# Twenty-two unused f32 products on TensorE ahead of the wait for the ranks

## The chip, the cores and the metric

The kernel runs on one core of one Trainium2 chip. The metric is the device time of one execution in microseconds (us); lower is better. The median of three runs of the kernel before is 2611.15 us (2604.75 to 2613.42).

## What is computed

Two models run one after the other on 512 tokens of width 1024. The first has two layers (attention beside a convolution, then an expert-choice mixture), the second one layer. The change lies in the mixture of the first model, so it runs twice per execution:

```
logits = jnp.einsum('bsd,de->bse', h, w_router).astype(jnp.float32)
aff = jax.nn.softmax(logits, axis=-1)
gate, idx = lax.top_k(aff.transpose(0, 2, 1), cap)      # 16 experts, 64 tokens each
xe = jax.vmap(lambda hb, ib: hb[ib])(h, idx)
hid = jax.nn.silu(jnp.einsum('becd,edf->becf', xe, w_gate)) * jnp.einsum('becd,edf->becf', xe, w_up)
ye = jnp.einsum('becf,efd->becd', hid, w_down) * gate[..., None].astype(h.dtype)
return zeros((S, D)).at[idx].add(ye)
```

All weights and the activations are f32.

## The kernel before

`layer` (L288) writes one program per engine; a loop on the device runs it twice (`nc.Fori(0, DEPTH)`, L2862). Engines meet at semaphores, and the order on each engine is the order in which the code is written. No planner is involved.

The token tile `xT` holds the tokens as 128 features by 512 tokens, eight tiles deep, in f32. After the output projection and the router's logits, TensorE transposes `xT` in eight groups of four (`turn_rows`, L772), so that ScalarE can write the tokens row by row (`htok_ev`, L1038 and L1039), and it transposes the affinities (L779, `affT_done`). On VectorE the top 64 tokens of each of 16 experts are then found in eight rounds of the eight largest values (L1299, L1301), numbered by a scan (L1306) and masked (L1308, `rank_ready`). TensorE waits for `rank_ready` (L783), transposes the ranks with four small products (L785, `rankT_done`), and VectorE builds from them the one-hot matrix of the first pair of experts (`build`, L1313, `s_built`). With it TensorE gathers the tokens of that pair: `gather(0)` is 16 matmuls, alternately of L795 and L796, 8 for each half of the width. `gates(0)` (L810, L812) and `turn_tokens(0)` (L804) follow, VectorE scales and shifts the result (L1327, L1329), and the first expert starts (`expert`, L837 for gate and up, L864 for down).

The weights of an expert come in six chunks of 2 MB on SyncE's one queue (L446). Eight chunks are issued before the first expert starts: six of expert 0 and two of expert 1. Each further one waits for `chunk_used`, which TensorE signals after every chunk (`expert`, for the first time after the first four products of both halves). PSUM bank 0 is read last by L1274 before this place, and is written next by `gather(0)`.

Line names for matmuls: the operand marked `fp32r` or named `_r` is a rounded f32; `ident` (in the tensor `const`) and `xT` are plain f32. In the profile one L795 or L796 matmul is one record; the plain f32 product of the convolution's sum, L737 (four per layer, `ones` by `acc`, 128x512), is of the same kind and shape as the products of the change.

Of the kernel before, what the change touches and what calls it, by code (L numbers as in the profile page):

```python
# [14 lines left out]
KT = D // P  # L15
# [272 lines left out]
def layer(nc, A, sem, M, l, ahead):  # L288


    ps, const, xT, ring, scr = M["ps"], M["const"], M["xT"], M["ring"], M["scr"]
    ident, rot = const[:, C_IDENT:C_IDENT + P], const[:, C_ROT:C_ROT + P]
# [118 lines left out]
    with nc.Block() as block:  # L411
# [98 lines left out]
        def _(pe):  # L510
# [255 lines left out]
            def turn_rows(i):  # L766
                t, g = i // 2, i % 2
                if i >= 4:
                    pe.wait_ge(htok_ev, i - 3)
                for b in range(4):  # L770
                    kt = 4 * g + b
                    mm = pe.transpose(ps[:, 2 + i % 4, b * P:(b + 1) * P], xT[:, kt, t * P:(t + 1) * P], ident)  # L772
                mm.then_inc(htok_mm, 1)
# [6 lines left out]
            mm.then_inc(affT_done, 1)  # L780
            for i in range(4, 2 * TT):
                turn_rows(i)
            pe.wait_ge(rank_ready, 1)  # L783
            for t in range(TT):
                mm = pe.transpose(ps[:, 7, t * EXPERTS:(t + 1) * EXPERTS], rankm[:, t * P:(t + 1) * P].bitcast(F32), ident[0:EXPERTS, 0:EXPERTS])  # L785
# [2136 lines left out]
```

## Time and profile before

| | us |
|---|---|
| median of three runs | 2611.15 |
| the profiled execution's own time | 2608.86 |
| its span | 2607.0 |
| TensorE busy | 2362.6 (91%) |
| VectorE busy | 1134.7 (44%) |
| ScalarE busy | 911.7 (35%) |
| DMA, mean over the span | 250 GB/s |
| TensorE clock, mean granted share of full speed | 0.973 |

Busy time is the sum over an engine's instructions; matmuls overlap at their ends, so that the distance between two starts, and not a duration, is what one costs in a dense row. A clock of 1.00 is 2.4 GHz, 0.50 is 1.2 GHz.

### The profile page before, as it was taken

The page shows a single profiled execution, that of the slowest core. Times are in us where ns is not written, and L with a number is a line of the kernel's source. Part 1 is how long each engine was busy: PE and PEld are TensorE (multiplying, and loading weights), DVE is VectorE, ACT ScalarE, POOL GpSimd, SP SyncE. Part 2 cuts the span into 40 slices and gives each one's busy share as a digit, 9 for nine tenths or more (in the row PEclk, how much of TensorE's full clock was granted, in tenths as well). Part 3 has the DMA queues.
Part 4 walks back from the last instruction along what each step waited for, and adds up shares of the span by engine and source line. Part 5 has one row for each costly group of instructions (what it writes and reads, how often), then busy time and mean ns, then how long its engine had stood idle before and what let it go on. Part 6 is the DMA issues. An engine that isn't in the chain of part 4 may idle for free. (4 is left out here: it accounts for less than half of the span.)

```text
span 2607.0 us, 31029 instructions
## 1 busy us (share of the span) xinstructions
PE 2362.6 (91%) x12565; PEld 1482.3 (57%) x12565; DVE 1134.7 (44%) x1678; ACT 911.7 (35%) x1228; POOL 241.9 (9%) x114
## 2 busy tenths in 40 slices
PE   6999799888887999799888888999999899989997
PEld 5735533333335835543333328887788777767776
DVE  4984312111214984321112125656612112458997
ACT  3256211111114256211111116656622234247775
POOL 0000100000000000100000005000244322200000
PEclk8999899999998989899999999999999999989999
DMA  9702499999999503399999995423123421149995
GB/s 347 277 1 100 159 388 409 410 410 410 410 408 356 211 0 119 153 409 409 410 410 409 410 405 166 162 81 97 65 85 89 133 76 54 49 159 379 369 372 215
DMA packets 276595, 650.47 MB, mean 250 GB/s; under 512 B 12144, under 2 KB 110718, under 8 KB 276222
## 3 DMA queue, kind: packets, MB, share of 16 engines
q1 hardware_dynamic: 272756, 637.98, 65.1%
q0 software_dynamic: 2592, 7.87, 0.8%
q10 hardware_dynamic: 1130, 2.99, 0.3%
q8 instruction: 83, 1.36, 0.2%
q14 instruction: 34, 0.28, 0.0%
HBM read 641.99 MB, written 8.39 MB: 249 GB/s over the span
## 5 line engine op out<-in xcount | busy, mean ns | idle before, releaser
L837 PE MATMUL ps<-ring,hy 128*64 128x512 f32 x992 | 225.6, 596 | 49.7 <-DMA ring<-in_w_up 32.2
L837 PE MATMUL ps<-ring,scr 128*64 128x512 f32 x992 | 225.2, 596 | 37.3 <-DMA ring<-in_w_up 31.3
L1343 DVE TENSOR_TENSOR scr<-scr,ps 128x512 f32<-128x512 f32 x32 | 22.0, 687 | 541.2 <-PE ps L837 541.2
L864 PE MATMUL ps<-ring,scr 128*64 128x512 f32 x1024 | 227.2, 595 | 4.1 <-ACT scr L1054 2.7
L1609 POOL TENSOR_TENSOR raw_r<-raw,w_high 128x2048 fp32r<-128x2048 f32 (+1 forms) x38 | 164.6, 4342 | 463.5 <-ACT w_high L1876 463.5
L1631 PE MATMUL ps<-x_high,w_high 128*128 128x512 f32 x464 | 187.4, 404 | 7.3 <-DVE y L2272 7.3
L2752 DVE TENSOR_TENSOR ring_r<-ring,ring_high 128x2048 fp32r<-128x2048 f32 x77 | 173.0, 2285 | 28.3 <-ACT ring_high L2629 28.2
L1633 PE MATMUL ps<-x_high,raw_r 128*128 128x512 f32 x464 | 184.5, 398 | 0.0
L837 PEld LDWEIGHTS ps<-ring,hy 128*64 128x64 f32 x992 | 69.2, 137 | 202.3 <-issue 122.4
L1632 PE MATMUL ps<-xT_r,w_high 128*128 128x512 f32 x464 | 183.5, 396 | 0.0
L837 PEld LDWEIGHTS ps<-ring,scr 128*64 128x64 f32 x992 | 68.1, 137 | 188.4 <-issue 121.1
L1131 DVE SCALAR_TENSOR_TENSOR one_hot_T<-h_tok,convw,one_hot_T 128x512 f32<-128x512 f32 x240 | 166.3, 745 | 1.8
L2629 ACT ACTIVATE ring_high<-ring 128x2048 fp32r<-128x2048 f32 x77 | 144.0, 1917 | 31.8 <-DMA ring<-in_w_up 31.1
L864 PEld LDWEIGHTS ps<-ring,scr 128*64 128x64 f32 x1024 | 70.5, 137 | 141.1 <-issue 128.8
L1876 ACT ACTIVATE w_high<-raw 128x2048 fp32r<-128x2048 f32 (+1 forms) x58 | 105.9, 1826 | 96.2 <-DMA raw<-in_p_b 49.0
L1063 ACT ACTIVATE hy<-ps,gcol 64x512 f32<-64x512 f32 x64 | 43.6, 682 | 256.3 <-PE ps L864 255.9
L1631 PEld LDWEIGHTS ps<-x_high,w_high 128*128 128x128 f32 x464 | 87.8, 189 | 29.5 <-DVE y L2272 7.7
L1632 PEld LDWEIGHTS ps<-xT_r,w_high 128*128 128x128 f32 x464 | 87.9, 189 | 22.7 <-issue 2.2
L1633 PEld LDWEIGHTS ps<-x_high,raw_r 128*128 128x128 f32 x464 | 87.6, 189 | 19.5
L2542 PE MATMUL ps<-ring_high,xg_high 128*128 128x512 f32 x224 | 92.9, 415 | 2.9 <-DVE xg_low L2758 2.9
L1054 ACT ACTIVATE scr<-ps 128x512 f32<-128x512 f32 x32 | 19.1, 595 | 206.2 <-PE ps L849 206.2
L2544 PE MATMUL ps<-ring_high,xg_low 128*128 128x512 f32 x224 | 87.8, 392 | 0.0
(581 smaller groups left out, 4520.4 us busy)
## 6 DMA issues: line engine op xcount, KB each, us to landing
ring<-in_w_up SPq DMA_DIRECT2D x64, 2048.0 KB, 23.6
ring<-in_w_down SPq DMA_DIRECT2D x64, 2048.0 KB, 23.5
ring<-in_w_gate SPq DMA_DIRECT2D x60, 2048.0 KB, 23.3
ring<-in_w_up SPq DMA_DIRECT2D x56, 1024.0 KB, 6.9
ring<-in_w_ada SPq DMA_DIRECT2D x22, 2048.0 KB, 13.7
ring<-in_w_down SPq DMA_DIRECT2D x28, 1024.0 KB, 6.6
raw<-in_w_in SPq DMA_DIRECT2D x24, 1024.0 KB, 5.0
raw<-in_w_in SPq DMA_DIRECT2D x20, 512.0 KB, 5.2
```

The costliest lines, as they stand in the source:

```text
L837: mm = pe.matmul(ps[CAP * half:CAP * (half + 1), 1 + j // 2, :], x_e[j % 2][:, at_x:at_x + CAP], weights[:, k, half * HALF:(half + 1) * HA ...
L864: mm = pe.matmul(ps[CAP * half:CAP * (half + 1), 4, :], hidT[:, at_f:at_f + CAP], weights[:, k, half * HALF:(half + 1) * HALF], start=(j = ...
L1131: op = dve.scalar_tensor_tensor(acc[:, c, :], src, w, acc[:, c, :], ALU.mult, ALU.add)
L1609: pool.tensor_tensor(dst, src, high.bitcast(F32), ALU.subtract).then_inc(w_ready, 1)
L1631: pe.matmul(out, s_high, m_high, start=(n == 0), stop=False)
L1632: pe.matmul(out, s_high, m_low, start=False, stop=False)
L1633: mm = pe.matmul(out, s_low, m_high, start=False, stop=(n == len(terms) - 1))
L1876: act.activation(slot_of(w_high, n), landed_chunk(n), ACT.Copy).then_inc(w_split, 1)
L2542: pe.matmul(ps[:, n % 2, :], xh[i % 2][:, kt, :], h[:, k, :], start=(kt == 0), stop=False)
L2544: mm = pe.matmul(ps[:, n % 2, :], xl[i % 2][:, kt, :], h[:, k, :], start=False, stop=(kt == KT - 1))
L2629: act.activation(high[q], raw[q], ACT.Copy).then_inc(w_split, 1)
L2752: dve.tensor_tensor(low[q], raw[q], high[q].bitcast(F32), ALU.subtract).then_inc(w_ready, 1)
```

## The change

Between the last `turn_rows` and the wait for the ranks, TensorE is given 22 products, `ident` as the stationary matrix and a token tile as the moving one, each whole in itself, into PSUM bank 0. Nothing reads their result and no semaphore is signalled.

```
             for i in range(4, 2 * TT):
                 turn_rows(i)
+            for i in range(22):
+                pe.matmul(ps[:, 0, :], ident, xT[:, i % KT, :], start=True, stop=True)
             pe.wait_ge(rank_ready, 1)
             for t in range(TT):
                 mm = pe.transpose(ps[:, 7, t * EXPERTS:(t + 1) * EXPERTS], rankm[...], ident[0:EXPERTS, 0:EXPERTS])
```

## Rows read from the trace of the kernel before

**Rows 1.** The page's head and its first part: busy time by engine.
```profile
span 2607.0 us, 31029 instructions
PE 2362.6 (91%) x12565; PEld 1482.3 (57%) x12565; DVE 1134.7 (44%) x1678; ACT 911.7 (35%) x1228; POOL 241.9 (9%) x114
```
**Rows 2.** Timeline of TensorE, first layer: start, length, what, idle before it.
```profile
295.18 0.60 PE L779 MATMUL ps<-const,aff 128*16 128x128 f32 x4 [0.99 <-DVE aff L1293]
295.62 0.64 PE L772 MATMUL ps<-const,xT 128*128 128x128 f32 x4
...
299.07 0.66 PE L772 MATMUL ps<-const,xT 128*128 128x128 f32 x4 [0.50 <-ACT one_hot_T_r L1039]
310.19 0.60 PE L785 MATMUL ps<-const,krg_r 16*128 16x16 f32 x4 [10.47 <-DVE krg_r L1308]
311.67 0.77 PE L795 MATMUL ps<-one_hot_T_r,scr_r 128*128 128x512 f32 x1 [0.87 <-DVE scr_r L1313]
312.23 0.63 PE L796 MATMUL ps<-h_tok_r,scr_r 128*128 128x512 f32 x1
312.66 0.63 PE L795 MATMUL ps<-one_hot_T_r,scr_r 128*128 128x512 f32 x1
...
317.76 0.39 PE L795 MATMUL ps<-one_hot_T_r,scr_r 128*128 128x512 f32 x1
317.99 0.40 PE L796 MATMUL ps<-h_tok_r,scr_r 128*128 128x512 f32 x1
318.23 0.95 PE L810 MATMUL ps<-aff,scr_r 128*128 128x2 f32 x8
...
321.70 3.65 PE L837 MATMUL ps<-ring,scr 128*64 128x512 f32 x16 [1.07 <-DVE scr L1329]
```
**Rows 3.** Timeline of VectorE at the same place.
```profile
309.46 0.68 DVE L1308 TENSOR_TENSOR krg_r<-hy 16x512 fp32r<-16x512 f32 x1
310.83 0.69 DVE L1313 TENSOR_TENSOR scr_r<-const,ps 128x512 fp32r<-128x512 f32 x1 [0.70 <-PE ps L785]
```
**Rows 4.** Timeline of TensorE, second layer.
```profile
1078.30 0.66 PE L772 MATMUL ps<-const,xT 128*128 128x128 f32 x4 [0.50 <-ACT one_hot_T_r L1039]
1089.42 0.60 PE L785 MATMUL ps<-const,krg_r 16*128 16x16 f32 x4 [10.46 <-DVE krg_r L1308]
1090.90 0.77 PE L795 MATMUL ps<-one_hot_T_r,scr_r 128*128 128x512 f32 x1 [0.87 <-DVE scr_r L1313]
...
1096.99 0.95 PE L810 MATMUL ps<-aff,scr_r 128*128 128x2 f32 x8
```
**Rows 5.** Windows: length, busy by engine, PEclk, DMA share, GB/s.
```profile
290.00:299.00 9.00, 5.42 (x58) 3.87 (x50) 5.22 (x17) 7.13 (x14) 3.37 (x3) 1.00 0.95 363
300.00:302.00 2.00, 0.00 (x0) 0.00 (x0) 1.90 (x5) 2.00 (x5) 2.00 (x3) 0.66 1.01 403
317.00:318.00 1.00, 1.00 (x5) 0.78 (x4) 0.00 (x0) 0.00 (x0) 0.00 (x0) 0.64 0.00 0
1082.00:1084.00 2.00, 0.00 (x0) 0.00 (x0) 1.91 (x4) 0.96 (x3) 2.00 (x3) 0.58 1.03 410
1095.00:1096.00 1.00, 1.00 (x4) 0.81 (x3) 0.00 (x0) 0.28 (x1) 0.00 (x0) 0.52 0.00 0
```
**Rows 6.** Timeline of TensorE at the convolution's sum, first layer, full clock.
```profile
194.20 3.60 PE L737 MATMUL ps<-one_hot_T,ones 128*128 128x512 f32 x8
197.64 1.02 PE L707 MATMUL ps<-ring 128*128 128x512 f32 x2
```
**Rows 7.** Groups by line and form: names, shapes, count, busy us, mean ns, idle.
```profile
L795 PE MATMUL ps<-one_hot_T_r,scr_r 128*128 128x512 f32 x128 | 54.9, 429 | 1.7 <-DVE scr_r L1313 1.7
...
L737 PE MATMUL ps<-one_hot_T,ones 128*128 128x512 f32 x16 | 7.2, 592 | 0.0
```
**Rows 8.** Timeline of SyncE's queue, 311 to 326 us: all that it issued.
```profile
325.40 0.37 SPq L446 DMA_DIRECT2D ring<-in_w_up  x1
```
**Rows 9.** Windows after the wait and in the loop of experts, columns as in rows 5.
```profile
320.00:322.00 2.00, 0.93 (x8) 0.59 (x8) 1.74 (x3) 0.32 (x1) 0.00 (x0) 1.00 0.00 0
...
480.00:520.00 40.00, 34.84 (x158) 12.58 (x154) 9.43 (x18) 5.42 (x8) 0.00 (x0) 1.00 1.03 410
```
**Rows 10.** Waits of SyncE's queue, 300 to 345 us: total, times, longest.
```profile
SPq L446 <- PE ps L837: 40.5, 4, 31.6
```

More of the change, by code:

```diff
@@ L782, in _ @@
                 turn_rows(i)
+            for i in range(22):
+                pe.matmul(ps[:, 0, :], ident, xT[:, i % KT, :], start=True, stop=True)
             pe.wait_ge(rank_ready, 1)
```

## Prediction

> **What bounds the kernel now.** I read the page's busy times first [rows 1]: TensorE is busy for 91% of the span, so anything that keeps it longer in one place is likely to be paid. An average says nothing about this place, so the next view is TensorE's timeline around the edit [rows 2]. The reader is to see there a hole: the last group of token transposes starts at 299.07, the next instruction, the transposes of the ranks, at 310.19, after 10.47 us of idle time that VectorE's L1308 ended. VectorE's timeline [rows 3] has L1308 ending at 309.46 + 0.68 = 310.14. In the second layer the hole is the same, 10.46 us [rows 4]. So at this place the path runs through VectorE's ranking, and TensorE has time to give away, but only so much.
>
> Then the clock [rows 5]. It is 1.00 up to the hole. In the window 300 to 302 its mean is 0.66, which with the two levels 1.00 and 0.50 puts the fall at 300.64, some 1 us after TensorE went idle; in the second layer the mean of 0.58 puts it at 1082.32, over 3 us after. It comes back at 317.72 (mean 0.64 in 317 to 318) and at 1095.96 (0.52 in 1095 to 1096), in the middle of the gather. The gather therefore runs mostly at 1.2 GHz: one start to the next is 312.66 - 312.23 = 0.43 us, against 317.99 - 317.76 = 0.23 us at 2.4 GHz [rows 2].
>
> Last, what follows. Eight chunks of weights lie ready, and SyncE's queue issues nothing more until 325.40 [rows 8]; the wait that ends there is 31.6 us long and is TensorE's L837 [rows 10]. The DMA share is 0.00 from 320 to 322 and then 1.03 at 410 GB/s in the loop of experts [rows 9]. Two chains thus start at the first expert, both from TensorE: its own, and the DMA stream, which is full to the end of the layer. Neither can make up what is lost before it.
>
> **The change, part by part.** It adds 22 products per layer, 44 in all, and removes and moves nothing. No wait and no DMA is added; the products stand in TensorE's queue between the last token transposes and the wait for the ranks.
>
> *When they start.* Four transposes occupy the engine for 295.62 - 295.18 = 0.44 us until the next instruction starts [rows 2]. So the first product starts at 299.07 + 0.44 = 299.51 in the first layer and at 1078.30 + 0.44 = 1078.74 in the second [rows 4]. Bank 0 is free then and `xT` is not being written, so nothing holds them.
>
> *What one costs.* The convolution's sum is four plain f32 products of 128x512 per layer, eight in all, and it shows as 16 records [rows 7]: two records for one product. The rounded gather matmuls show as one each (8 pairs x 2 halves x 4 x 2 layers = 128, [rows 7]). The reader is not to take the mean of 592 ns as the cost of a product; the ends overlap, and there are two records. The first layer's eight records start at 194.20 and what follows starts at 197.64 [rows 6]: 3.44 us for four products, 0.86 us each, at full clock. 22 products are 22 x 0.86 = 18.92 us. They are the same kind and shape, with a whole 128x128 stationary matrix, so I take this row. The lower bound is one record for a product, 0.43 us, 9.46 us in all; the upper one is the half clock throughout, by the gather's ratio 0.43 / 0.23 = 1.87: 1.61 us each, 35.4 us in all.
>
> *What lies beside other work and what on the path.* The products end (that is, what follows can start) at 299.51 + 18.92 = 318.43 in the first layer. The ranks are there at 310.14, so some half of the products, about 10.6 us of them, is hidden under the ranking on VectorE, and the rest is on the path: L785 starts at 318.43 instead of 310.19, 8.24 us late. In the second layer it starts at 1078.74 + 18.92 = 1097.66 instead of 1089.42, also 8.24 us late. Behind them on TensorE stand L785, the gather, the gates and the first expert, and VectorE waits for L785 to build the one-hot matrix. So the stall for the ranks goes, and what is late next is VectorE's L1313, then everything.
>
> *What they give back.* TensorE is no longer idle for 10 us, so I expect the clock to stay at 1.00 through the products, and through the 0.87 us in which VectorE builds. From L785 to the first gather matmul it is 311.67 - 310.19 = 1.48 us either way, since what lies between is VectorE's 0.69 us and hand-overs. The gather took 318.23 - 311.67 = 6.56 us in the first layer and 1096.99 - 1090.90 = 6.09 us in the second. At full clock it is 16 x 0.23 = 3.68 us, with 0.1 us more for the first one, whose step (0.56) was longer than the later ones (0.43) [rows 2]: 3.78 us. That gives back 2.78 and 2.31 us. From L810 on the clock was already full before. The bounds of this term are nothing (the clock falls again anyway) and these values.
>
> *Sum.* First layer 8.24 - 2.78 = +5.46, second 8.24 - 2.31 = +5.93, together +11.4 us. Against the profiled execution's own time, 2608.86 (span 2607.0 and 1.9 around it), this is 2620.3 us. The median of the runs shown lies 2.3 us above that execution, 2611.15, and from it the sum is 2622.5. I forecast 2622.
>
> The clock is where the Trainium skill is worth weighing. In rows 5 the clock stayed at 1.00 from 290 to 299, although TensorE was busy for 5.42 of 9 us there, mostly with transposes, and it fell 1 us after these ended. The Trainium skill, "TensorE: Matmul & The Clock Gate", Part 4 (PE-mode transpose), says that transposes do not count as activity for the clock as matmuls do. By that rule the products might begin just as the clock is about to fall, and run at first at the half level; without the rule they keep it up from the first. The sum would be as in the second rival below by the one, and 2620.3 by the other.
>
> **The rivals.**
>
> *The products fit into the hole.* This is the side where the kernel becomes faster. If a product costs one record, 0.43 us, the 22 end at 299.51 + 9.46 = 308.97, before the ranks at 310.14. Nothing is late, and the gather runs at full clock: -2.78 - 2.31 = -5.1 us, 2603.8 us from the profiled execution, 2606 from the median. The point from which it decides is the hole and the gain together: a product may cost up to (310.19 - 299.51 + 2.55) / 22 = 0.60 us before the change loses. For it: the stationary matrix is the same in all, and 22 x 0.43 us is about the hole. Against it: rows 6 and 7, where the stationary matrix is the same in all four as well and a product still takes 0.86 us. The Trainium skill, same page, "Back-to-back issue gap", gives about 131 ns for a matmul of 512 columns in a long stream; this trace has 0.23 us for a rounded one at full clock, so here the rule does not hold, and by it (an estimate: four such steps for an f32 product) the 22 would take 11.5 us, a loss of under 1 us per layer against a gain of 2.5.
>
> *The clock falls during the products.* The fall at 300.64 came about 1 us after the last transposes, so what went before it counted for little. If the clock falls there in spite of the products, dense work needs the time that the gather needed to bring it back: 317.72 - 311.67 = 6.05 us and 1095.96 - 1090.90 = 5.06 us. At 1.2 GHz half of that is lost: 3.0 + 2.5 = 5.5 us more, 2625.8 from the profiled execution, about 2628 from the median. For it: the fall was quick in the first layer. Against it: in the second layer it was over 3 us behind, and products follow on the transposes without a gap. The extreme is that this kind of product never holds the clock: 35.4 us per layer, 299.51 + 35.4 = 334.9, 24.7 us late twice and no gain, 2658 us. Against that stands the loop of experts, plain f32 products at a clock of 1.00 [rows 9].
>
> *The delay is absorbed.* If the DMA stream did not start from the first expert but from something earlier, a TensorE late by 5.5 us would be waited out in the loop, where it has about 5 idle us in 40 [rows 9]. The time would stay at 2609 to 2611. Against it: the queue's issue at 325.40 [rows 8] is released by L837 itself [rows 10], and moves with it.
>
> **How the numbers follow.** Forecast 0.74; clock falls for a while 0.11, for the whole of the products 0.03; products fit 0.06; absorbed 0.06. The forecast's own range is 2616 to 2627: the median's own uncertainty is some 4 us, the start and the step of a product some 0.5 us per layer. The range for 8 in 10 takes in the fall for a while and a part of the absorbed case: 2612 to 2630. What a measurement of this kernel can tell from no change is 0.3%, 7.8 us. The forecast of +11.4 us is 0.44%, and with a few us of spread between runs about one sixth of its chance falls under that bound. So faster 0.06, same 0.06 + 0.13 = 0.19, slower 0.75.
>
> **What the changed profile would show.** Two records for each product, 88 in all, the first at about 0.44 us behind the last transposes, at steps of 0.43 us; no idle time ahead of L785, which starts some 19.4 us behind the last group of L772 instead of 11.1; L1313 on VectorE with a wait of 8.9 us instead of 0.7; a clock of 1.00 in every window from there to L837; a gather of 3.8 us; the first expert 5.5 to 5.9 us later counted from the last token transposes, SyncE's next issue later by the same, and the loop of experts as long as before. The prediction is wrong if the products take 44 records or steps well under 0.43 us, if the clock shows 0.50 in any of these windows, or if L837 starts later but the layer doesn't end later.

## The result and the profile after

The kernel with the 22 products takes 2621.25 us (median of 8 runs), the kernel before 2608.84 us beside it. The ratio is 1.0047, 95% interval 1.0035 to 1.0059, which is 12.3 us slower (9.1 to 15.4). The forecast was 2622 us, from a sum of +11.4 us.

The page of the profiled execution after, first part:
```profile
span 2617.1 us, 31205 instructions
...
PE 2396.2 (92%) x12653; PEld 1497.2 (57%) x12653; DVE 1136.7 (43%) x1678; ACT 912.4 (35%) x1228; POOL 243.1 (9%) x114
```
TensorE has 88 more records than in [rows 1], two for each of 44 products, and is busy 33.6 us longer. No other engine changed its work.

TensorE's timeline after at the two places (L784 the products, L787 the transposes of the ranks, L797 and L798 the gather, L812 the gates, L839 the first expert; the view ends inside the last row, whose whole group is again 16 records in 3.65 us):
```profile
300.75 1.02 PE L772 MATMUL ps<-const,xT 128*128 128x128 f32 x4 [0.50 <-ACT one_hot_T_r L1041]
301.56 20.42 PE L784 MATMUL ps<-xT,const 128*128 128x512 f32 x44
321.90 0.42 PE L787 MATMUL ps<-const,krg_r 16*128 16x16 f32 x4
323.20 0.47 PE L797 MATMUL ps<-one_hot_T_r,scr_r 128*128 128x512 f32 x1 [0.87 <-DVE scr_r L1315]
...
326.93 0.95 PE L812 MATMUL ps<-aff,scr_r 128*128 128x2 f32 x8
...
330.40 3.65 PE L839 MATMUL ps<-ring,scr 128*64 128x512 f32 x16 [1.07 <-DVE scr L1331]
...
1084.70 0.66 PE L772 MATMUL ps<-const,xT 128*128 128x128 f32 x4 [0.50 <-ACT one_hot_T_r L1041]
1085.19 19.05 PE L784 MATMUL ps<-xT,const 128*128 128x512 f32 x44
1104.17 0.42 PE L787 MATMUL ps<-const,krg_r 16*128 16x16 f32 x4
1105.46 0.47 PE L797 MATMUL ps<-one_hot_T_r,scr_r 128*128 128x512 f32 x1 [0.87 <-DVE scr_r L1315]
...
1109.21 0.95 PE L812 MATMUL ps<-aff,scr_r 128*128 128x2 f32 x8
...
1112.68 2.80 PE L839 MATMUL ps<-ring,scr 128*64 128x512 f32 x12 [1.07 <-DVE scr L1331]
```
The wait ahead of the ranks' transposes ([rows 2], 10.47 us) is gone. Counted from the start of the last group of token transposes (L772), all times in us:

| | first layer before | after | second layer before | after |
|---|---|---|---|---|
| ranks' transposes start | 11.12 | 21.15 | 11.12 | 19.47 |
| from there to the gather | 1.48 | 1.30 | 1.48 | 1.29 |
| gather | 6.56 | 3.73 | 6.09 | 3.75 |
| first expert starts | 22.63 | 29.65 | (L837 at 1100.46) 22.16 | 27.98 |

So the two places cost 7.02 + 5.82 = 12.84 us. The spans differ by 10.1 us. The rest lies elsewhere and has both signs: the last transposes of the first layer come 1.68 us later (300.75 against 299.07), the stretch from the first expert to the second layer's last transposes is 2.30 us shorter (754.30 against 756.60), and the rest of the span 2.12 us shorter. These stretches have no edit. In the eleven traces of this document the last transposes of the first layer start at 296.90 to 302.39, and the stretch to the second layer's takes 754.30 to 759.62 us, so they vary by such amounts. The table's 12.84 us is therefore the change's own part, and 10.1 us is one pair of executions.

VectorE's timeline after shows who waits now:
```profile
311.14 0.68 DVE L1310 TENSOR_TENSOR krg_r<-hy 16x512 fp32r<-16x512 f32 x1
322.37 0.69 DVE L1315 TENSOR_TENSOR scr_r<-const,ps 128x512 fp32r<-128x512 f32 x1 [10.55 <-PE ps L787]
```
The ranks are ready at 311.82, and VectorE then idles for 10.55 us (0.70 in [rows 3]) until TensorE is through with the products.

SyncE's queue after, all that it issued from 326 to 337 us, and where the next layer's loads begin:
```profile
334.10 0.37 SPq L446 DMA_DIRECT2D ring<-in_w_up  x1
...
772.54 19.81 SPq L142 DMA_DIRECT2D ring<-in_w_ada  x3
```
Before, the first was at 325.40 [rows 8]: 8.70 us earlier, just as the first expert's start (321.70 against 330.40). Of the 8.70 us, 7.02 are the change's, and 1.68 were there before its place. The second line was this in the kernel before:
```profile
764.27 19.80 SPq L142 DMA_DIRECT2D ring<-in_w_ada  x3
```
It is 8.27 us later now. The delay has gone through the 440 us of the experts nearly whole.

The clock, in windows of the kernel after (columns as in [rows 5]):
```profile
300.00:301.00 1.00, 0.50 (x5) 0.26 (x4) 0.97 (x2) 1.00 (x3) 1.00 (x1) 0.95 1.03 422
301.00:302.00 1.00, 1.00 (x5) 0.90 (x4) 0.93 (x4) 1.00 (x3) 1.00 (x2) 0.50 1.06 430
...
303.00:304.00 1.00, 1.00 (x2) 0.34 (x1) 0.96 (x2) 1.00 (x4) 1.00 (x2) 0.50 0.98 393
304.00:305.00 1.00, 1.00 (x3) 0.48 (x2) 0.93 (x4) 1.00 (x3) 1.00 (x2) 0.85 1.03 414
```
In the first layer it fell at about 300.9, while the last transposes ran, and was back at 304.3. That is why the products took 20.42 us there and 19.05 in the second layer, where no window shows less than 1.00.

### The profile page after: what moved, and what is told of

It is laid out like the page before. It is cut to its first block and busy times, and to the rows that moved or that the text cites. A ratio compares the mean times of both kernels' runs of the same rounds, so it can differ in the third digit from the quotient of the medians.

```text
span 2617.1 us, 31205 instructions
## 1 busy us (share of the span) xinstructions
PE 2396.2 (92%) x12653; PEld 1497.2 (57%) x12653; DVE 1136.7 (43%) x1678; ACT 912.4 (35%) x1228; POOL 243.1 (9%) x114
## 5 line engine op out<-in xcount | busy, mean ns | idle before, releaser
L839 PE MATMUL ps<-ring,hy 128*64 128x512 f32 x992 | 225.6, 596 | 49.6 <-DMA ring<-in_w_up 32.2
L839 PE MATMUL ps<-ring,scr 128*64 128x512 f32 x992 | 225.2, 596 | 37.2 <-DMA ring<-in_w_up 31.4
L839 PEld LDWEIGHTS ps<-ring,hy 128*64 128x64 f32 x992 | 69.3, 137 | 202.0 <-issue 122.1
L839 PEld LDWEIGHTS ps<-ring,scr 128*64 128x64 f32 x992 | 68.1, 137 | 188.3 <-issue 121.0
L1047 ACT ACTIVATE hy<-ps 128x512 f32<-128x512 f32 x32 | 19.2, 599 | 207.7 <-PE ps L798 207.7
```

What stands on the lines that cost most here:

```text
L839: mm = pe.matmul(ps[CAP * half:CAP * (half + 1), 1 + j // 2, :], x_e[j % 2][:, at_x:at_x + CAP], weights[:, k, half * HALF:(half + 1) * HA ...
```

## The experiments

Expectations name the line numbers of their kernels. "Distance" is the time from the start of the last group of token transposes to the first expert, first and second layer; before it was 22.63 and 22.16 us. Each ratio is taken against executions of the kernel before beside it: one set of them for 11, 44, 22 behind the wait and the transposes, a second for 16, the nine and the first spread, a third for the last two rows. The ratios are medians over executions, and the distances are of one execution each.

| kernel | ratio (95%) | in us | distances | both against before |
|---|---|---|---|---|
| 22 products (the change) | 1.0047 (1.0035 to 1.0059) | +12.3 | 29.65, 27.98 | +12.8 |
| 11 products | 0.9981 (0.9972 to 0.9990) | -5.0 | 19.63, 20.20 | -5.0 |
| 16 products | 1.0014 (1.0004 to 1.0024) | +3.7 | 24.52, 22.83 | +2.6 |
| 44 products | 1.0188 (1.0172 to 1.0203) | +49 | 48.55, 48.56 | +52.3 |
| 22 behind the wait | 1.0147 (1.0132 to 1.0163) | +38 | 41.68, 40.11 | +37.0 |
| 88 transposes | 0.9970 (0.9959 to 0.9981) | -7.8 | 20.33, 20.33 | -4.1 |
| 9 products, each with a wait | 0.9976 (0.9966 to 0.9986) | -6.3 | 21.21, 19.62 | -4.0 |
| 15 products, spread | 0.9975 (0.9966 to 0.9984) | -6.5 | 19.12, 19.14 | -6.5 |
| 14 products, spread | 0.9985 (0.9974 to 0.9996) | -3.9 | 19.13, 20.75 | -4.9 |
| 15 spread, once more | 0.9982 (0.9970 to 0.9993) | -4.7 | 19.12, 19.13 | -6.5 |

In the spread kernels the last transposes start some 0.5 us later than elsewhere, so their distances are that much too good in each layer (-5.5, -3.9 and -5.5 us without it).

The distances end where the first expert starts, and three layers lost more just behind that point. The clock fell once more there, and the expert's first 16 records, 3.65 us elsewhere, took 5.28 us (16 products, first layer), 5.16 us (44, second) and 5.35 us (88 transposes, first). In the first of them, on TensorE's timeline, in the windows (columns as in [rows 5]) and in SyncE's queue:
```profile
322.37 5.28 PE L839 MATMUL ps<-ring,scr 128*64 128x512 f32 x16 [1.07 <-DVE scr L1331]
...
322.00:323.00 1.00, 0.64 (x2) 0.30 (x4) 0.97 (x3) 0.00 (x0) 0.00 (x0) 0.64 0.00 0
...
327.69 3.81 SPq L446 DMA_DIRECT2D ring<-in_w_up  x2
```
SyncE's next issue comes 5.32 us behind the expert's start, 3.70 in the kernel with 22. With these 1.6, 1.5 and 1.7 us the sums of the traces are +4.2 us for 16 products, +53.8 for 44 and -2.4 for the 88 transposes.

**11 products.**
```
-            for i in range(22):
+            for i in range(11):
```


> Eleven f32 products in each layer instead of 22, same place. My theory (a product costs 0.86 us of TensorE at full clock and only what reaches beyond the ranks is paid): the 11 need 9.5 us, so they end about 1 us before the ranks, nothing is late, and the clock is 1.00 through the gather, which takes 3.8 us instead of 6.1 to 6.6. Sum 5.1 to 5.6 us faster than before, a ratio of about 0.998. L785's counterpart starts at the same distance behind the last token transposes as before, 11.1 us. Rival (the products cost something beside their time, or the clock falls all the same): no gain, or a loss of up to 3 us, ratio 1.000 to 1.001.

The kernel is faster than the one before. TensorE's timeline of the first layer (distance 19.63):
```profile
299.96 0.66 PE L772 MATMUL ps<-const,xT 128*128 128x128 f32 x4 [0.50 <-ACT one_hot_T_r L1041]
300.45 9.61 PE L784 MATMUL ps<-xT,const 128*128 128x512 f32 x22
311.07 0.42 PE L787 MATMUL ps<-const,krg_r 16*128 16x16 f32 x4 [1.02 <-DVE krg_r L1310]
```
The ranks' transposes start 11.11 us behind the last group, as before, and still wait 1.02 us for VectorE; the gather took 3.76 us. In the second layer the clock fell for 3.4 us just at the start, the products took 11.12 us and made L787 0.6 us late. The rival is out: the products cost nothing that shows while they fit.

**44 products.** As above, with `range(44)`.

> 44 f32 products in each layer instead of 22. My theory: every product beyond the first ten or so is paid in full to the end of the kernel, 0.86 us each: 22 more in each of two layers are 37.8 us on top of the loss of 22, about 50 us slower than before, ratio 1.019. Rival (the loop of experts, where TensorE has idle time, takes up part of the delay): clearly less than 37.8 us on top, such as half, ratio 1.012.

The ratio is 1.0188 where 1.019 was expected. Against 22 products the distances grew by 18.90 and 20.58 us for 22 x 0.86 = 18.9 us of products; the 1.7 us too many in the second layer are again a fall of the clock (39.56 us for 44 products, 0.90 each). In time it is 49 - 12.3 = 37 us, 37.8 expected, and half of that by the rival. The trace has 53.8 - 12.8 = 41.0 us, but it is of the slowest of the four executions, with the lowest mean clock (2668.42 us, median 2661.29; 0.974 against 0.976 to 0.980). So the loop of experts absorbs little or nothing.

**22 products behind the wait.**
```
+            pe.wait_ge(rank_ready, 1)
             for i in range(22):
                 pe.matmul(ps[:, 0, :], ident, xT[:, i % KT, :], start=True, stop=True)
-            pe.wait_ge(rank_ready, 1)
```


> The 22 products stand behind the wait for the ranks instead of ahead of it. My theory: nothing covers them any more. They start at 1.2 GHz, as the gather did, so 18.9 us plus some 2 to 3 us of slow clock come on the path in each layer, and the gather behind them is at full clock (2.3 to 2.8 us back): +18.5 us per layer, +37 us in all, ratio 1.014. The difference to the kernel with the 22 ahead of the wait, some 25 us, is the cover of the hole, twice 10.6 us, plus the slow start. Rival (the loss of 22 has nothing to do with the cover): about the same time as with the 22 ahead, ratio 1.005.

The ratio is 1.0147, 26 us slower than with the same products ahead of the wait. So the cover is real. The products begin at the slow clock and take 22.1 us in the first layer:
```profile
308.02 22.15 PE L785 MATMUL ps<-xT,const 128*128 128x512 f32 x44 [10.09 <-DVE krg_r L1310]
330.11 0.42 PE L787 MATMUL ps<-const,krg_r 16*128 16x16 f32 x4
```

**88 transposes instead of products.** Against the kernel with 22:
```
-            for i in range(22):
-                pe.matmul(ps[:, 0, :], ident, xT[:, i % KT, :], start=True, stop=True)
+            for i in range(88):
+                pe.transpose(ps[:, 0, (i % 4) * P:(i % 4 + 1) * P], xT[:, i % KT, 0:P], ident)
```


> In place of the 22 products 88 unused transposes of 128x128 in each layer, about 9.6 us of TensorE at the 0.11 us each that the token transposes take. Theory A (transposes hold the clock as matmuls do): clock 1.00 through the hole, the gather takes 3.8 us, 5 us faster than before. Theory B (transposes do not hold it): the clock falls to 0.50 during them, the rest of them runs at half speed and ends up to 9 us late, and the gather is slow at first: up to 15 us slower than before, the trace shows 0.50 soon after they begin.

Windows of this kernel from 298 us, when only these transposes ran from 298.62 to 309.7:
```profile
298.00:299.00 1.00, 1.00 (x6) 1.00 (x6) 0.96 (x3) 1.00 (x3) 1.00 (x2) 0.50 1.02 410
...
301.00:302.00 1.00, 1.00 (x9) 1.00 (x8) 0.96 (x3) 1.00 (x3) 1.00 (x2) 0.79 1.00 401
302.00:303.00 1.00, 1.00 (x12) 1.00 (x10) 0.93 (x4) 0.51 (x2) 1.00 (x1) 1.00 1.03 410
...
307.00:308.00 1.00, 1.00 (x12) 1.00 (x11) 1.00 (x1) 0.00 (x0) 0.00 (x0) 1.00 1.05 418
```
The clock fell at the start, in both layers, and then came back and stayed while TensorE did nothing but transposes. Theory B is out: here a dense row of transposes was enough for the clock to come back and to stay for the remaining 8 us, in both layers. The fall, while the last token transposes ran, made the row 11.1 us long and the ranks' transposes 0.7 us late. The Trainium skill, "TensorE: Matmul & The Clock Gate", Part 4 (PE-mode transpose), has it that transposes don't engage the full clock; for these f32 transposes the measurement says otherwise.

This kernel's time is the lowest ratio of the first set. The interval (-5.0 to -10.7) does not reach the -2.4 us of the trace. That trace shows three falls of the clock, and without any the best two layers of the other kernels (11 products first, nine products second) make -3.00 - 2.54 = -5.5 us, which is inside. The traced execution had the lowest mean clock of the seven (0.975, the others 0.976 to 0.979), so the others probably had fewer falls; they have no trace.

**16 products.** As above, with `range(16)`.

> 16 products in each layer. My theory: they need 13.8 us, are 3.1 us late for the ranks, and the clock that they keep up gives back 2.5 us in the gather and 0.2 us in the transposes of the ranks: within 1 us of the kernel before, ratio 1.000, half a us per layer on either side. Rival (the clock gives back nothing that reaches the end, and the gain seen with 11 products came from elsewhere): 6 us slower, ratio 1.0024.

It came out at +3.7 us (1.0 to 6.3). I expected less than 1 us, so this is a miss, and the time alone is compatible with the rival's +6. The trace tells them apart: the gathers took 3.73 and 3.75 us, and the second layer, where the clock did not fall, is 0.67 us later than before. The first is 1.89 us later at the first expert's start, where it fell during the products, and 1.6 us more behind it, where it fell again: +4.2 us in all. One product more in each layer is 2 x 0.86 = 1.7 us. By this estimate the break-even is near 16 - 3.7 / 1.7 = 14 products (12 to 15 by the interval), not 16, because the falls were left out of the sum.

**Nine products, each waiting for a step of the ranking.**
```
-            for i in range(22):
+            for i in range(9):
+                pe.wait_ge(d_step, 32 + 2 * i)
```


> Nine products in each layer, each held back until a further round of VectorE's ranking is done, so that they can't be late for the ranks, with about 0.6 us of idle time between two. If such a thinner row holds the clock, the gather takes 3.8 us, L787 starts 11.1 us behind the last token transposes, and the kernel is 5 to 6 us faster than before, as with 11 in a row. If it doesn't, the windows show 0.50 and the gather begins at the slow clock: 0 to 2 us faster.

The waits did not make the thin row that I expected. In the second layer six of the nine products ran in one dense row, and only two gaps of 0.37 us followed. In the first there is no gap at all, since the clock had fallen behind the token transposes and the nine took 9.46 us:
```profile
303.22 9.46 PE L785 MATMUL ps<-xT,const 128*128 128x512 f32 x18
```
In the second layer the clock held and the gather took 3.73 us. In the first it fell a second time, in the gather, which took 5.32 us; windows of that stretch:
```profile
314.00:316.00 2.00, 1.19 (x5) 1.05 (x6) 1.17 (x5) 0.00 (x0) 0.00 (x0) 1.00 0.48 193
316.00:318.00 2.00, 2.00 (x6) 1.51 (x5) 0.00 (x0) 0.58 (x1) 0.00 (x0) 0.54 0.01 4
```
The fall at 316.1 comes when the gather has been dense for over 1 us; what went before it were the idle 0.84 and 0.87 us around the ranks' transposes. Eight other layers of the kernels here have two such gaps (0.6 to 1.0 us and 0.87 us), and the clock fell in the gather in one of them. So this run doesn't test a thin row. It shows nine products that are never late and gain 6.3 us (3.7 to 8.9), level with the 11, and a second fall in one layer of two.

**Fifteen products, spread.** The token transposes themselves wait 0.50 us for ScalarE three times. Here one product stands in each of these gaps:
```
             for i in range(4, 2 * TT):
                 turn_rows(i)
+                if i < 2 * TT - 1:
+                    pe.matmul(ps[:, 0, :], ident, xT[:, i % KT, :], start=True, stop=True)
+            for i in range(11):
+                pe.matmul(ps[:, 0, :], ident, xT[:, i % KT, :], start=True, stop=True)
             pe.wait_ge(rank_ready, 1)
...
             turn_tokens(0)
+            pe.matmul(ps[:, 3, :], ident, xT[:, 0, :], start=True, stop=True)
             expert(0, 0, True, False)
```


> Fifteen products in each layer: one behind each of the token transposes 5 to 7 (where TensorE waits 0.5 us for ScalarE each time), eleven ahead of the wait for the ranks, and one behind the turned tokens of the first pair, where TensorE waits 1.07 us. With the eleven alone the clock fell for 3.4 us right after the transposes in one layer of the two. Theory (it is the thin stretch of transposes that lets it fall): no window from the transposes to the first expert shows 0.50, L839 starts 19.6 to 20.1 us behind the last group of transposes in both layers, 5 to 6 us faster than before. Rival (the falls come at any place and have nothing to do with it): 0.50 in one of the layers as before.

Windows of this kernel, one of each layer over the hole:
```profile
300.00:310.00 10.00, 10.00 (x27) 4.44 (x25) 9.55 (x20) 4.41 (x9) 6.20 (x6) 1.00 1.03 410
...
1076.00:1086.00 10.00, 9.01 (x25) 3.78 (x23) 9.09 (x18) 2.72 (x6) 4.48 (x4) 1.00 1.03 410
```
There is no fall, and the time (2603.94 us beside 2610.22) is level with that of the nine products (2604.48).

**Two more looks at the spread.** Once without the last product, once unchanged.

> The kernel with 15 products without the last one, that behind the turned tokens: three between the token transposes and eleven behind them. Two more layers in which to see whether the products between the transposes keep the clock from falling there. Theory: 1.00 in all windows from 10 us ahead of the last transposes to the gather's end, in both layers; L839 19.1 us behind the last group; 5 to 6 us faster than before. Rival (that both layers of the earlier run were without a fall was chance, since about half of the layers are without one anyway): 0.50 within 1 us of the last group in at least one layer.

> The same kernel as with 15 products once more, two further layers for the same question. Theory: again no window at 0.50 between the transposes and the first expert, L839 19.1 us behind the last group in both layers, ratio 0.9975. Rival: a fall in one of the layers, L839 some 0.6 us later there or its first matmuls longer than 3.65 us.

With unused work placed directly behind the transposes, the clock fell within 1 us of the last group's start in 8 of 12 layers (one of two with 22, 11, 16 and the nine; both with 44 and with the 88 transposes). It also did in both layers of the kernel with the products behind the wait, 0.1 and 0.3 us after that start, where no product follows for 10 us. With products between the transposes it fell there in none of 6. If the placing made no difference, 8 falls in 18 layers would leave these 6 without one about once in 90 times (an estimate from these counts). So the falls very probably come from the thin stretch of transposes, and work behind it comes too late to prevent them. But with 14 it fell once later, in the gather of the second layer, and the kernel gained 3.9 us where 5 to 6 were expected:
```profile
1089.00:1090.00 1.00, 0.85 (x4) 0.74 (x5) 0.52 (x5) 0.00 (x0) 0.00 (x0) 1.00 0.08 29
1090.00:1091.00 1.00, 1.00 (x5) 0.82 (x4) 0.00 (x0) 0.00 (x0) 0.00 (x0) 0.77 0.03 12
1091.00:1092.00 1.00, 1.00 (x4) 0.71 (x4) 0.00 (x0) 0.23 (x1) 0.00 (x0) 0.50 0.00 0
```
TensorE had been idle for 0.61 and 0.87 us shortly before it. The spread kernels are faster than the kernel before in all three comparisons; whether they beat 11 in a row by the 1 to 2 us that a fall costs is too little for these intervals.

## Why the prediction was right

The sum was +11.4 us; the time gave +12.3 (9.1 to 15.4) and the distances +12.84. The forecast was right in its cost, its wait and its path. One step, that the clock stays up, failed in one layer of two: the clock showed 0.50 there, which the prediction had named as a sign of being wrong. The time stayed close because such a fall costs 1.7 us and no more.

*Two records, 0.86 us for a product.* Right. 22 products took 1104.17 - 1085.19 = 18.98 us until the next start where the clock held, 18.92 predicted. The rival of the cheap product is refuted in all kernels. The Trainium skill, "TensorE: Matmul & The Clock Gate", "Back-to-back issue gap", has 131 ns for a matmul of 512 columns in a stream; here a record of the f32 product stepped by 0.43 us and one of the rounded gather by 0.23.

*The cover.* Right: in the second layer the ranks' transposes came 19.47 - 11.12 = 8.35 us late (8.24 predicted), so 18.98 - 8.35 = 10.63 us of the products are free. 11 products lose nothing in the layer where the clock held, and 22 behind the wait lose 26 us more than 22 ahead of it.

*What they give back.* Right in the gather: 2.83 and 2.34 us against 2.78 and 2.31. I left out that the ranks' transposes and what lies behind them ran at the slow clock before: 1.48 became 1.30 and 1.29, 0.37 us in all.

*The clock stays up.* Half right. In the second layer it did, and the loss was 5.82 us (5.93 predicted). In the first it fell, as in the second rival. The rival's counterargument, that products follow on the transposes without a gap, does not hold: the fall comes while the last transposes run or just as they end. But it cost 21.15 - 19.47 = 1.7 us and not the 3.0 that I took from the gather's slow time, since the clock was back after 3.4 us, and not after 6. With it the loss was 7.02 us, 5.46 predicted. The experiments make such a fall the usual case: 8 layers of 12. The sum should have had about 1 us per layer for it, which makes 11.4 - 0.4 + 2 = 13 us. Nor did the prediction have the falls at the first expert (three layers, 1.5 to 1.7 us each); the kernel of the change had none in its trace.

*It reaches the end.* Right. SyncE's queue restarts later by the same 8.70 us as the first expert, the next layer's loads by 8.27, and 22 further products cost 37 us of their 37.8.

## What to carry to other kernels

An engine's idle time can take unused work only up to its length. A busy row keeps the clock up for what follows, but that gain stays only while the row is inside the idle time or little longer: here 11 products bring 5 us, 16 lose 3.7, 22 lose 12. Price such work by the distance between starts in a row of the same kind, count the records per product (two for plain f32), and leave a margin for a fall of the clock. If a thin stretch stands ahead of the hole, fill that one first. Follow the trace past the point where the edit's effect seems to end: here a second fall stood just behind it.

## What the runs showed of the hardware

- The clock can fall while TensorE is working thinly. It fell during token transposes with 0.50 us of idle time between the groups (within 1 us of the last group's start in 10 of the 16 layers that had no product between the groups), in the middle of a dense gather that two idle gaps of 0.6 to 0.9 us preceded (two layers of nine with such gaps), and at the first expert, behind 1.07 us of idle time (three layers).
- Where dense work followed at once, the half level lasted about 3.4 us each time. Where TensorE went idle for 10 us, it lasted 17.1 us in the first layer and 13.6 in the second (the kernel before, and that with the products behind the wait).
- With f32 transposes of 128x128 in a dense row, 0.11 us each, the clock came back after 3.4 us and stayed at 1.00 for the remaining 8 us, in both layers.
